# Half of each head's probability tiles turned by VectorE and a DMA instead of TensorE, with the scalings shared anew

## The reference, cut to what matters

```python
def one_block(qblk):
    s = jnp.einsum('bqhd,bkhd->bhqk', qblk, k).astype(F32) * scale
    p = jax.nn.softmax(s, axis=-1).astype(v.dtype)
    return jnp.einsum('bhqk,bkhd->bqhd', p, v)
```

## Time and profile before

| | |
|---|---|
| median of 3 runs | 1644.71 us (1644.7 to 1644.83) |
| span of the profiled execution | 1645.5 us |
| PE busy | 1633.9 us (99%) |
| DVE busy | 1043.6 us (63%) |
| ACT busy | 571.0 us (35%) |
| POOL busy | 1026.5 us (62%) |
| heads 0 to 15 | 113 to 317 us of the span |

### The profile page before, as it was taken

The page is one execution under the profiler, slowest core; times in us unless marked ns, Lnnn a source line. Parts: engine busy times, 40 slices in busy tenths (PEclk is TensorE's granted clock), DMA queues, the critical chain, the costliest instruction groups (busy, mean ns, idle before and its releaser), DMA issues.

```text
span 1645.5 us, 24018 instructions
## 1 busy us (share of the span) xinstructions
PE 1633.9 (99%) x8950; PEld 1364.2 (83%) x8950; DVE 1043.6 (63%) x1537; ACT 571.0 (35%) x1017; POOL 1026.5 (62%) x656
## 2 busy tenths in 40 slices
PE   9999999999999999999999999999999999999998
PEld 7887778798888888889887798888888898888887
DVE  3567777677877865635487566655558359746173
ACT  3467777633233232203344243222222121123111
POOL 3455766656666766575579456666676645567663
PEclk9999999999999999999999999999999999999999
DMA  9234335232269863435322233344434253223332
GB/s 371 87 90 129 111 106 165 79 93 96 89 211 320 298 225 103 141 137 172 120 90 65 77 99 102 125 156 140 153 106 143 97 214 120 65 84 103 91 101 90
DMA packets 59095, 220.61 MB, mean 134 GB/s; under 512 B 6849, under 2 KB 9153, under 8 KB 55682
## 3 DMA queue, kind: packets, MB, share of 16 engines
q1 hardware_dynamic: 53826, 204.96, 38.2%
q10 hardware_dynamic: 5184, 14.49, 2.3%
HBM read 201.07 MB, written 14.16 MB: 131 GB/s over the span
## 4 chain that ended last, share of the span: by engine, by line
PE 95%; DVE 4%; ACT 0%; issue 0%; DMA 0%; DVEq 0%; SPq 0%; ACTq 0%
PE PS L2444 28%; PE PS L2446 28%; PE PS L2445 28%; PE PS L2821 3%; PE PS L2783 2%; PE PS L1012 1%; PE PS L2430 1%; PE PS L1785 1%; PE PS L2595 1%; DVE SC L3572 0%; DVE WA L1990 0%; PE PS L1791 0%; DVE MR L3522 0%; PE PS L2720 0%; PE PS L2721 0%
## 5 line engine op out<-in xcount | busy, mean ns | idle before, releaser
L2354 POOL TENSOR_TENSOR WL<-RAW,WH 128x1024 fp32r<-128x1024 f32 (+3 forms) x211 | 542.8, 2572 | 17.6
L2444 PE MATMUL PS<-HH,WH 128*128 128x512 f32 (+1 forms) x1340 | 507.5, 379 | 0.0
L2446 PE MATMUL PS<-HH,WL 128*128 128x512 f32 (+1 forms) x1340 | 502.9, 375 | 0.0
L2445 PE MATMUL PS<-HL,WH 128*128 128x512 f32 (+1 forms) x1340 | 502.9, 375 | 0.0
L2351 POOL TENSOR_SCALAR WH<-RAW 128x1024 fp32r<-128x1024 f32 (+3 forms) x211 | 239.4, 1134 | 287.8 <-PE PS L2446 276.5
L2444 PEld LDWEIGHTS PS<-HH,WH 128*128 128x128 f32 x1340 | 252.2, 188 | 50.7 <-issue 6.2
L2446 PEld LDWEIGHTS PS<-HH,WL 128*128 128x128 f32 x1340 | 252.2, 188 | 45.9
L2445 PEld LDWEIGHTS PS<-HL,WH 128*128 128x128 f32 x1340 | 252.3, 188 | 43.9
L2379 POOL TENSOR_SCALAR PR<-PR,SC 128x768 f32<-128x768 f32 x47 | 107.3, 2292 | 66.7 <-DVE SC L3579 66.3
L2444 PE MATMUL PS<-HIDH,WH 128*128 128x512 f32 (+1 forms) x396 | 145.3, 367 | 0.0
L2445 PE MATMUL PS<-HIDL,WH 128*128 128x512 f32 (+1 forms) x396 | 144.8, 366 | 0.0
(11 more groups left out here) (532 smaller groups left out, 2894.6 us busy)
## 6 DMA issues: line engine op xcount, KB each, us to landing
RAW<-in_wup SPq DMA_DIRECT2D x88, 512.0 KB, 3.6
MRF<-in_modw SPq DMA_DIRECT2D x52, 512.0 KB, 4.8
RAW<-in_wdn SPq DMA_DIRECT2D x32, 704.0 KB, 4.1
MR<-in_modw SPq DMA_DIRECT2D x28, 512.0 KB, 3.6
RAW<-in_whin SPq DMA_DIRECT2D x24, 512.0 KB, 3.5
MK<-in_modk SPq DMA_DIRECT2D x8, 1024.0 KB, 10.9
RAW<-in_wo SPq DMA_DIRECT2D x8, 512.0 KB, 4.2
hy_hs<-HST ACTq DMA_DIRECT2D x4, 1024.0 KB, 4.0
```

Source lines behind the costliest of these rows:

```text
L2354: pool.tensor_tensor(WL[s][:, 0:n], raw[:, 0:n], WH[s][:, 0:n].bitcast(F32), ALU.subtract).then_inc(tile_split, 1)
L2444: pe.matmul(out, wh, xh, start=first, stop=False)
L2445: pe.matmul(out, wh, xl, start=False, stop=False)
L2446: return pe.matmul(out, wl, xh, start=False, stop=last)
```

## The change

Tiles 0 and 1 of each head (BLOCKED = 2) are no longer transposed by TensorE. ScalarE writes their exponentials in another column order, GpSimd scales them, VectorE transposes them in place in blocks of 32x32, and SP stores both to DRAM (d_blocks) and loads them back with one DMA of 128 partitions into PB, in which the value product reads them. ScalarE scales tiles 2 and 3. Tiles 2 and 3 are transposed by TensorE in three groups of four, copied to PT by three copies. The early rows are spread anew: five before head 0, two in head 0, two in each odd head from 1 to 13, three in head 14, four in head 15. prepare_angles moves behind head(15). SP's loop is written out with the new DMAs in it. Some semaphores are merged to make room (not shown).

```diff
+BLOCKED = 2
+PRE_ROWS = 5
+        PB = r.put("PB", [P, BLOCKED, 4, 6, 32])
+        PT = r.put("PT", [P, 6, P * (4 - BLOCKED)])
+        d_blocks = nc.dram_tensor("pr_blocks", (2, BLOCKED, P, LK), F32).ap()
...
+            def blocks_out(h, qt):
+                sp.wait_ge(S["turned"], BLOCKED * h + qt + 1)
+                sp.dma_start(d_blocks[h % 2, qt, :, :], PR[h % 2][:, qt, :]).then_inc(S["blocks_out"], 16)
+            def blocks_in(h):
+                sp.wait_ge(S["pv"], h + 1)
+                sp.wait_ge(S["blocks_out"], 16 * BLOCKED * (h + 1))
+                sp.dma_start(PB[:, :, :, :, :].rearrange("p i m t j -> p (i m) (t j)"),
+                             d_blocks[h % 2].rearrange("i (m k) (c x) -> (k c) (i m) x", m=4, c=4)
+                             ).then_inc(S["blocks_in"], 16)
...
+            for h in range(16):
+                if h % 2 and h < 11:
+                    head_weights(h // 2 + 3)
+                elif h == 11 or h == 13:
+                    ring("wo", a["wo"], h // 2 - 5)
+                if h % 2 and h < 15:
+                    mod_load(16 + PRE_ROWS + 1 + h)
+                    mod_load(16 + PRE_ROWS + 2 + h)
+                if h % 4 == 3 and h < 12:
+                    rope_move(h + 1, 2)
+                elif h % 4 == 0 and 0 < h < 13:
+                    rope_move(h + 2, 2)
+                elif h == 14:
+                    sp.wait_ge(S["rope"], 512)
+                    x_again(0)
+                    mod_load(16 + EARLY - 7)
+                elif h == 15:
+                    mod_load(16 + EARLY - 5)
+                    mod_load(16 + EARLY - 4)
+                for qt in range(BLOCKED):
+                    blocks_out(h, qt)
+                if h > 13:
+                    mod_load(16 + EARLY + 3 * h - 48)
+                blocks_in(h)
+                if h == 0:
+                    for r in range(4, PRE_ROWS + 2):
+                        mod_load(16 + r)
+            x_again(1)
+            mod_load(16 + EARLY - 2)
+            mod_load(16 + EARLY - 1)
...
             def normalise(h):
-                for qt in range(3 if h else 2):
+                for qt in range(2):
...
+            def turn(h, n):
+                if n == 0:
                     if h == 0:
                         pe.wait_ge(S["kready"], key_hi_at(0) + 2)
-                pe.wait_ge(S["pt"], 7 * h + max(kt - 1, 0) + 1)
-                turn_blocks(h, kt, 0, 4)
+                    else:
+                        pe.wait_ge(S["pt"], 5 * h + 1)
+                if n == 2:
+                    pe.wait_ge(S["pt"], 5 * h + 2)
+                for kt in (2 * n, 2 * n + 1):
+                    for qt in range(BLOCKED, 4):
+                        q = (kt % 2) * 256 + (qt - BLOCKED) * P
+                        m = pe.transpose(PS[:, 6 + n % 2, q:q + P], PR[h % 2][:, qt, kt * P:(kt + 1) * P], IDENT[:, :])
+                m.then_inc(S["s_tr"], 1)
...
+                pe.wait_ge(S["blocks_in"], 16 * (h + 1))
                 for kt in range(6):
-                    pe.wait_ge(S["pt"], 7 * h + kt + 2)
-                    for half in range(2):
-                        m = pe.matmul(PS[VH * half:VH * half + VH, out_bank(h), 0:256], V[:, kt, v],
-                                      PT[:, kt, tok(half)], start=kt == 0, stop=kt == 5)
+                    pe.wait_ge(S["pt"], 5 * h + kt // 2 + 2)
+                    pe.matmul(PS[0:VH, out_bank(h), 0:256].rearrange("p (i m j) -> p i m j", i=2, m=4), V[:, kt, v],
+                              PB[:, :, :, kt, :], start=kt == 0, stop=kt == 5)
+                    m = pe.matmul(PS[VH:2 * VH, out_bank(h), 0:256], V[:, kt, v], PT[:, kt, :], start=kt == 0, stop=kt == 5)
...
@@ TensorE, head(h)
-                if h:
-                    first_turns(h)
-                else:
-                    turn(h, 0)
-                    turn(h, 1)
+                turn(h, 0)
+                turn(h, 1)
...
-                    turn(h, qt + 2)
+                    if qt == 1:
+                        turn(h, 2)
@@ ScalarE
+                out, src = PR[h % 2][:, qt, :], wide(2 * (qt % 2), LK)
+                if qt < BLOCKED:
+                    out, src = out.rearrange("p (c t j) -> p c t j", c=4, t=6), src.rearrange("p (t j c) -> p c t j", t=6, c=4)
...
+                act.copy(PT[:, 2 * n:2 * n + 2, :].rearrange("p k q -> p (k q)"), bank(6 + n % 2)).then_inc(S["pt"], 1)
...
                 if h < 15:
+                    normalise(h + 1, i, per, 2)
                     normalise(h + 1, i, per)
@@ VectorE
+            def block_turn(h, qt, i=0, per=0):
+                dve.wait_ge(S["pnorm"], i * (2 * per) + (2 * h + qt + 1))
+                dve.transpose(PR[h % 2][:, qt, :], PR[h % 2][:, qt, :]).then_inc(S["turned"], 1)
...
                 if h < 15:
                     inverse_sum(h + 1, 3, i, per)
+                    block_turn(h + 1, 0, i, per)
...
                 if h % 2:
                     row(1)
+                if h in (14, 15):
+                    row(2)
+                if h == 15:
+                    row(3)
+                if h < 15:
+                    block_turn(h + 1, 1, i, per)
                 out_lo(h, i, per)
...
             maximum(0, 2)
+            pre_row(0)
             maximum(0, 3)
             inverse_sum(0, 2)
+            pre_row(1)
             inverse_sum(0, 3)
-            head(0, range(0, 2))
+            for qt in range(BLOCKED):
+                block_turn(0, qt)
+            for r in range(2, PRE_ROWS):
+                pre_row(r)
+            head(0)
...
-            head(13, range(26, 28))
-            head(14, ())
+            head(13)
+            head(14)
+            head(15)
+            dve.wait_ge(S["mod_used"], 16 + EARLY)
             prepare_angles()
-            head(15, ())
```

More of the change, by code:

```diff
@@ L2243, in _, with x_again @@
             rope_move(2, 2)
[L2244 to L2259, removed]
+            for r in range(4):
+                mod_load(16 + r)
+                if r == 1:
+                    head_weights(2)
+            def x_again(k):
                 sp.wait_ge(S["s_ready"], 56 + 8 * k)
                 sp.dma_start(X[:, 4 * k:4 * k + 4, :], a["x"][:, 4 * k:4 * k + 4, :]).then_inc(S[f"x_in{k}"], 16)
+            for h in range(16):
[24 more added lines that the diff above has]
+                    for r in range(4, PRE_ROWS + 2):
+                        mod_load(16 + r)
+            x_again(1)
+            mod_load(16 + EARLY - 2)
+            mod_load(16 + EARLY - 1)
             with sp.Fori(0, 3) as i:
@@ L3123, in head @@
                 turn_copy(h, 0, i, per)
+                if h % 4 == 0 and per:
+                    mod_store(i)
                 for kt in range(1, 6):
-                    turn_copy(h, kt, i, per)
+                    if kt == 1 or kt == 3:
+                        turn_copy(h, (kt + 1) // 2, i, per)
                     if kt == 1 and h % 4 == 3 and h < 12:
@@ L3145, in head @@
                     query_hi(3)
-                if h % 2 and h < 14:
-                    mod_store(2 * h - 2, 4, i, 2 * per)
             rope_hi(0)
@@ L3589, in out_lo, with head @@
                                       ALU.subtract).then_inc(S["olo"], 1)
-            def head(h, rows, i=0, per=0):
+            def block_turn(h, qt, i=0, per=0):
+                dve.wait_ge(S["pnorm"], i * (2 * per) + (2 * h + qt + 1))
+                dve.transpose(PR[h % 2][:, qt, :], PR[h % 2][:, qt, :]).then_inc(S["turned"], 1)
+            def head(h, i=0, per=0):
                 def row(k):
-                    if rows:
-                        if k == 0 and h % 2 == 0 and h:
-                            dve.wait_ge(S["modx"], i * (per // 2) + h // 2)
-                        mod_rows(rows[k], i, 2 * per, MACC[:, rows[k] % 4:rows[k] % 4 + 1], MR, CB[:, :])
+                    if h == 0:
+                        r = PRE_ROWS + k
+                    elif h > 13:
+                        r = EARLY - 7 + 3 * (h - 14) + k
+                    elif h % 2:
+                        r = PRE_ROWS + 2 + h - 1 + k
+                    else:
+                        return
+                    if per:
+                        if h == 1 and k == 0:
+                            dve.wait_ge(S["modx"], i + 1)
+                        mod_row(r, MACC[:, r - PRE_ROWS - 2:r - PRE_ROWS - 1], i, per)
+                    else:
+                        mod_row(r, MOD[:, 16 + r:17 + r])
                 late_row = h % 4 == 0 and 0 < h <= 12
@@ L3606, in head @@
                     inverse_sum(h + 1, 0, i, per)
-                    row(0)
                     maximum(h + 1, 2, i, per)
@@ L3610, in head @@
                     query_lo(h + 2, i, per)
-                    row(1)
                     maximum(h + 1, 3, i, per)
@@ L3647, in head @@
                     query_lo(3)
[L3649 removed]
+            dve.wait_ge(S["side_in"], 80)
             rope(0)
```

99 lines of the change are left out of this document (41 added, 58 removed).

## The result

The changed kernel takes 1679.91 us (median of four, 1676.96 to 1681.69) against 1644.77 for the one before: a ratio of 1.0209, 95% interval 1.0195 to 1.0224. It is 35 us slower; the forecast was 7.5 slower, and its range ended at 1668. The profiled execution spans 1679.8 us. Ratios are of fast runs alone; one run of the kernel before, of 5823.9 us in the last batch, is left out.

The account below looks back on a forecast made before the run. TensorE, busy 1633.9 of 1645.5 us, was taken as the bound. Terms: -21 (transposes) + 11.7 (heads 1 to 13) + 5.5 (head 0) + 2.4 + 4.4 (heads 14, 15) + 4.5 (end) = +7.5, so 1652.2 us; range 1631 to 1668.

Parts of the forecast that it names:

- -21 us: All 16 heads: fewer transposes and change-overs on TensorE save 1.2 to 1.3 us a head, 21 us in all.
- the exponential's pace: Heads 4, 8, 12: with one projection between four scores, maximum and exponential set the pace; 0.8 us of the saving lost.
- The block trip in the steady heads: Value product waits for blocks through DRAM (trip 7.2 us): 1.9 us after heads 2, 6, 10, 0.2 after heads 4, 8, 12.
- Rival (b): VectorE's transposes and the DRAM trip come 2 us sooner, no head waits for blocks: faster, 1634 us; chance 0.27.
- (c): 768-byte runs or queueing make the DRAM trip 10 us, so odd heads, 14 and 15 wait longer: 1672 us; chance 0.14.
- ScalarE's two scalings: Next head's transposes wait for both scalings behind the last exponential: 0.5 to 1.3 us each, 0.3 where value was held.
- Head 0: The fifth early row loads behind PB and delays maximum(1, 0) to 120.2 us: 5.5 us lost including its own saving.
- Heads 14 and 15: Head 14 waits for blocks and exponentials, 2.4 us; head 15's trip makes value(15) 3.1 later, 4.4 with its saving.
- The end: After value(15): late rows 26 and 27, then prepare_angles (7.8 us), delay the residuals and linear("wo", 4); cost 4.5 us.
- (d): Tile path works, the two ends cost half, steady heads 1 us per four less: 1645 us, no change; chance 0.13.
- The base: The profiled span, 1645.5 us, is 0.8 over the median 1644.71; the sum, a difference, was added to the median.
- The signs to look for: TensorE waits at transposes and value products, PB load 4 to 5 us, maximum(1, 0) near 120, gap before linear("wo", 4).

Follow-up runs that it names:

- prize kernel: The kernel before with TensorE's transposes of tiles 0 and 1 left out and nothing added; ratio 0.9977 to the kernel before, 3.8 us faster.
- e4_free: The changed kernel with the value product reading PT for both halves, neither reading nor waiting for the blocks in PB; ratio 1.0212 to the kernel before.

## Why the prediction was wrong, point by point

1. **"Every microsecond taken off TensorE counts, if nothing else comes late in its place."** This is the step that failed: what comes late in its place was priced far too low. The -21 us stood at the head of the sum as if it were sure. The work was over-sized a little (4.3 us of four heads, not 5.2; the change-overs before the value product were counted as saved and are not), but the larger error is what stood behind it. With the transposes gone and nothing added, 3.8 us are won by the medians and 6.0 in the traces; four heads lose 2.7 of the 4.1 us taken off, 8.8 us over heads 1 to 13, where the sum had 0.8 of four heads for this, 2.6 in all. With the waits that the new steps added, heads 1 to 13 cost 8.2 us where the sum had them save 5.2. The page says 99% busy; it doesn't say how much slack the steps behind have. I had priced the exponential's pace only in heads 4, 8 and 12 (0.8 us, and the trace has 1.4 and 1.0 us there), and the lost cover of out_lo and key_lo not at all: 3.8 and 2.3 us of waits in the changed kernel, the first and third largest in the prize kernel.
2. **The block trip in the steady heads (1.9 + 0.2 per four heads).** Its pieces were right: 0.97 us against 0.96, 2.3 against 2.4, 4.8 against 4.3 in the median. In heads 3 and 7 the trip was longer than the 7.2 us of the forecast: value starts 8.5 and 8.4 us after the end of the second transpose, 6.1 and 5.9 after PB's load was issued. The issues, taken at a quarter of a microsecond, last 0.33 and 0.37. The wait came in heads 3 and 7, 3.0 us in all. But taking it away (e4_free) gave nothing: beside it stood ScalarE's scaling, as late. Rival (b) priced the same trip shorter, so by the same run it could not have had the size that I gave it: one late step was varied where several stood level. What a longer trip (c) would cost no run shows.
3. **ScalarE's two scalings (0.7 per four heads).** Mechanism right, mis-sized: undoing one of them gave 5.6 us, 1.4 in four heads. That key_hi and out_hi stand behind it too fits the wait for out_lo that went, but was not tested alone.
4. **Head 0 (5.5, its own saving included: 4.2 net).** Right in mechanism and nearly in size: the maximum at 121.77 (forecast 120.2), score(1, 2) at 123.80 (122.1). Lost were 5.9 us, 7.0 from the first maximum on. Behind the wait of 7.05 us, which my sum had at its bare length, the next matmuls of 512 columns came in steps of 0.43 us instead of 0.23 for some 3 us (granted clock 0.50 from 123.8 to 126.8 us).
5. **Heads 14 and 15 (4.2 net).** 7.9. At the end of head 13 row 20 lasted 3.11 us instead of 1.2, beside a split of GpSimd, and the second transpose, out_lo(13) and the first maximum of head 15 stood behind it: 2.0 us of wait in head 14. In head 15 the matmuls behind the wait ran at 0.62.
6. **The end (4.5).** 12.3, the place that missed by most beside heads 1 to 13. I took 7.8 us for prepare_angles and held that it could shrink where GpSimd is idle. GpSimd was not idle: its splits stood behind the same queue (18.8 us without weights) and ran exactly beside it. The Trainium skill, page SBUF — State Buffer, section "SBUF: two separate sides", has the lock hold for VectorE's instructions in a two-port mode as well as for those with two SBUF inputs, and whichever engine starts first keeps it for its whole instruction. The trace agrees on the second point: TENSOR_SCALAR with one input and 16 columns began 0.19 us behind a split of 2.41 and ended 0.03 behind it, after 2.25 us. In which mode it ran the trace doesn't show. My forecast had read from that rule only that the chain may get shorter.
7. **The rivals.** Rival (b), faster with 1634 us, had 0.27; by the prize kernel 1639 to 1644 was the most that this change could give before other things are mended. Rival (c), 1672, is nearest in number, but its sign, a load of PB of over 7 us, didn't come (4.8 in the median, at most 5.8), so that its nearness is luck. In (d) the two ends cost half of mine; they cost more.
8. **The base.** The 0.8 us between span and median compare two different measures, as said at the result. The sum is a difference and isn't touched.

The signs to look for were well chosen: waits at the transposes by ScalarE, at PB in head 7, the maximum near 120. These were there. Head 11 had no wait for PB, and the gap expected before linear("wo", 4) came before output tile 3, 6.4 us. What was missing from the list was a bound of the whole: what is left if TensorE had nothing to transpose.

## What to carry to other kernels

Before a change that takes work off the bounding engine, go through the rows just behind that work on the other engines: each that ends less than the saved time before it is wanted takes its part of the gain. At 99% busy the neighbours may all be level with it, and here they left a fifth to a third of the saving. A new DMA on an in-order queue needs its place stated against every load that waits for someone (rows 4 and 5: 4.8 us; row 8: a wait of 3.4; the second row of heads 3, 7, 11 and 13: 3.8), and an order that is tuned by hand must be fitted again before the change is judged: this one was 2.1% slower as made and, with the moves of order and the last head back on TensorE, 0.34% faster.

## What the hardware showed that I had not expected

- Behind a wait of 2.0 to 7.1 us of TensorE the granted clock of the next 3 to 5 us was mostly 0.50 to 0.72 (0.50, that is 1.2 GHz, at 359.5 to 363; the means between are stretches with both levels). It can cost up to 2 us more than the wait: the ten residuals took 2.1 us less with dummy matmuls in the wait before them, which kept the clock at 1.00. The wait of 2.0 us in head 14 was followed by 0.72 (317 to 323 us) in the changed kernel and by 1.00 in the one with dummies, whose dummies come only later; in the kernel with the last head on TensorE one of 3.55 us was followed by 0.59, ones of 2.10 and 2.19 by 1.00. What decides is open.
- VectorE operations of 16 columns take 0.16 to 0.25 us, or 2.2 to 2.4 when they meet a two-input split of GpSimd (2.4 us), also those with one input. One-input operations of GpSimd (1.05 us) hold them too: in the kernel before a TENSOR_SCALAR of 16 columns takes 0.95 us from 312.98 beside one that runs from 312.85 to 313.90. Which ones meet is a matter of phase: it moved the ten residuals by 7.2 us between two kernels that differ in the place of three matmuls. A comparison of two orders below 0.5% says little on either unless this stage is looked at in both.
- The kernel before takes 1644.5 to 1649.1 us from one execution to the next; the kernels with waits spread over 1 to 7 us. Part of this lies ahead of the heads: in the profiled execution of the kernel before the first 96 us have a granted clock of 0.96, in that of the prize kernel, the same program up to there, 1.00. Differences of 2 us between two kernels rest on their traces, not on their times.
